# A second ordinary panel at the head of each feed-forward, splits of block sums in one piece, and weight sums held until the last square

## The chip, the cores and the metric

One core of a Trainium2 chip. The metric is the device time of one execution in microseconds. TensorE (PE) does matmuls, VectorE (DVE), ScalarE (ACT) and GpSimd (POOL) work on tiles of 128 partitions, and SP issues the loads. Each engine runs its own list of instructions in order; semaphores tie them together.

## What is computed

A block of two layers and a second block of one, in float32, over 512 tokens of width 1024: attention or a convolution or gated linear attention as the mixer of a layer, then a feed-forward. The change touches the three feed-forwards only, and what leads into them:

```python
def rmsnorm(x, g, eps=1e-6):
    xf = x.astype(jnp.float32)
    y = xf * lax.rsqrt(jnp.mean(xf * xf, axis=-1, keepdims=True) + eps)
    return (y * g.astype(jnp.float32)).astype(x.dtype)

def swiglu(h, w_gate, w_up, w_down):
    return (jax.nn.silu(h @ w_gate) * (h @ w_up)) @ w_down
...
        h = rmsnorm(x, ffn_norm[layer])
        x = x + swiglu(h, ffn_w_gate[layer], ffn_w_up[layer], ffn_w_down[layer])
```

The hidden width is 2816, which is 22 blocks of 128.

## The kernel before

Activations lie with their features on the partitions, 8 tiles of 128 x 512 (`x`). Every float32 product is made of three matmuls on halves of the mantissa: each operand is split into `hi` (a rounded copy, cast by ScalarE) and `lo` (the difference, by VectorE), and `hi·hi + lo·hi + hi·lo` is summed in PSUM. So each weight panel (128 x 2048, 1 MB) is loaded into one of two `raw` buffers, cast to `whi` by ScalarE and subtracted to `wlo` by VectorE. A load waits until the panel two before it is split. The mean square is not applied to the activations: `rstd` multiplies the results, so panels can start before it is known.

A feed-forward (`ffn`, f = 0, 1, 2) has 22 panels of gate and up weights, in two parts (12 and 10), each part followed by 8 down panels. Panel k holds the gate columns and the up columns of hidden block k. It is done in one of two ways:
- **ordinary** (panel 0): for each of the 8 feature tiles, gate and up, three matmuls of 512 columns: 48 in all, into two PSUM banks. Inside it stands the sum of squares (`sumsq`), from which ScalarE takes the root and VectorE the reciprocal (`inv`, `rstd`);
- **seven products** (panels 1 to 21): gate and up, and the first and second half of tokens, are treated as a 2 x 2 block product with seven products instead of eight, each of 4 x 3 matmuls of 256 columns: 84 in all, named B11, T1, B21, T2, B22, T3, T4 in the order of TensorE. They need sums of weights and sums of activations (**block sums**). GpSimd makes the weight sums of each panel with four additions (`weight_sums`; three can start once the panel has landed, the fourth after its `wlo`). ScalarE and VectorE split them (`hi_sum`, `lo_sum`, three of each a panel; `sw_hi`, `sw_lo`), ScalarE copies partial results between PSUM and SBUF (`take`), VectorE makes gate (`gate_first`, `gate_second`), up half (`up_second`, line 2050) and hidden (`hidden`), and T4 of a panel is issued after B11 of the next (`fourth`).

The block sums are made of x times its gain, once per feed-forward: `g12` and `n1` from tiles 0 to 3, `tt2`, `tt3`, `tt4` from tiles 4 to 7 (`summed`, line 1990, three sums a tile). They are split into `bt_hi` and `bt_lo` under the names T1, T2, T3; T4 goes into `act_hi` and `act_lo`.

The stage in front of a feed-forward (`late`) runs on VectorE and ScalarE while TensorE does the last matrix of the mixer: for each of 8 result tiles, x is updated (line 1998), squared and summed; the panel two ahead is split. Before the change `late` also does the block sums of tiles 4 and 5 and their splits T2 and T3 tile by tile (`part`), T1's split, then the first seven-product panel (`hi_panel`, `lo_panel`), the block sums of tiles 6 and 7 and their splits. `ffn` starts with panel 0 on TensorE; all that concerns it on VectorE (`whole_gate`, `whole_hidden`) is done inside step k = 1. The order on every engine is written out by hand, as these functions call one another. "Head" in what follows is the stretch from the first matmul of panel 0 to the start of steady work. "Panel 2" is the third one, and a panel's number is its k.

## Time and profile before

| | us |
|---|---|
| median of 3 runs | 1805.87 |
| lowest, highest | 1805.11, 1806.88 |
| profiled execution | 1802.89 |
| its span, first to last instruction | 1801.1 |
| TensorE busy | 1729.2 (96%) |
| VectorE busy | 1274.5 (71%) |
| ScalarE busy | 883.4 (49%) |
| GpSimd busy | 523.9 (29%) |
| three heads, first matmul of panel 0 | near 244, 785, 1374 |

The times come from executions of the whole program; the rows are of one profiled execution. Matmuls are pipelined: the durations shown overlap, and the distance of two starts is what one costs. TensorE's granted clock was 0.983 of full speed on average.

### The profile page before, as it was taken

What the parts mean: (1) busy time and instruction counts of PE and PEld (TensorE: products, weight loads), DVE (VectorE), ACT (ScalarE), POOL (GpSimd) and SP (SyncE); (2) the same over time, 40 slices, a digit from 0 to 9 for tenths busy, and PEclk for the clock granted to TensorE, in tenths of its full rate; (3) what the DMA queues carried; (4) which work ended last, traced back from release to release, by engine and by line L of the source; (5) the groups of instructions that cost most, each with busy time, mean ns of one, the idle gap of its engine ahead of it and who ended that gap; (6) DMA issues with size and microseconds to landing.
All of it is one profiled execution on the core that took longest, in us unless ns stands there. A gap on an engine that the chain in (4) does not pass through costs nothing. (4 is left out here: it accounts for less than half of the span.)

```text
span 1801.1 us, 27878 instructions
## 1 busy us (share of the span) xinstructions
PE 1729.2 (96%) x10773; PEld 1496.9 (83%) x10773; DVE 1274.5 (71%) x1792; ACT 883.4 (49%) x1355; POOL 523.9 (29%) x368
## 2 busy tenths in 40 slices
PE   7999989999999999989999999999998999999997
PEld 6776779988998865779988998788877998899876
DVE  8667688854875798688754776678758874477575
ACT  5338456732763312556732763433335673267342
POOL 1341125502540246225502540023301550255000
PEclk9899999999999999899999999999999999999998
...
DMA packets 284700, 169.01 MB, mean 94 GB/s; under 512 B 8288, under 2 KB 278528, under 8 KB 284576
## 3 DMA queue, kind: packets, MB, share of 16 engines
...
q8 instruction: 84, 1.38, 0.3%
...
## 5 line engine op out<-in xcount | busy, mean ns | idle before, releaser
L1036 PE MATMUL ps<-act_hi,whi 128*128 128x512 f32 x748 | 301.4, 403 | 22.3 <-DVE act_lo L1683 13.2
L1037 PE MATMUL ps<-act_lo,whi 128*128 128x512 f32 x748 | 294.3, 394 | 0.0
L1038 PE MATMUL ps<-act_hi,wlo 128*128 128x512 f32 x748 | 294.2, 393 | 0.0
L600 ACT ACTIVATE whi<-raw 128x2048 fp32r<-128x2048 f32 (+3 forms) x101 | 161.3, 1597 | 233.8 <-PE ps L1038 219.9
L1351 PE MATMUL ps<-act_hi,whi 128*128 128x256 f32 x756 | 215.4, 285 | 12.9 <-DVE t L2050 8.5
L1351 PE MATMUL ps<-act_lo,whi 128*128 128x256 f32 x756 | 213.6, 282 | 0.0
L1351 PE MATMUL ps<-act_hi,wlo 128*128 128x256 f32 x756 | 213.5, 282 | 0.0
L1651 DVE TENSOR_TENSOR wlo<-raw,whi 128x2048 fp32r<-128x2048 f32 (+3 forms) x93 | 183.1, 1969 | 38.0 <-ACT whi L600 37.7
L1036 PE MATMUL ps<-hid_hi,whi 128*128 128x512 f32 x528 | 209.8, 397 | 0.0
L1037 PE MATMUL ps<-hid_lo,whi 128*128 128x512 f32 x528 | 209.8, 397 | 0.0
L1038 PE MATMUL ps<-hid_hi,wlo 128*128 128x512 f32 x528 | 209.8, 397 | 0.0
L442 POOL TENSOR_TENSOR raw<-raw 128x512 f32<-128x512 f32 x63 | 82.7, 1313 | 402.3 <-DMA raw<-in_ffn_w_up_dram 240.6
L1036 PEld LDWEIGHTS ps<-act_hi,whi 128*128 128x128 f32 x748 | 142.4, 190 | 65.8 <-issue 27.6
L452 POOL TENSOR_TENSOR raw<-raw,ssum 128x512 f32<-128x512 f32 x63 | 102.2, 1623 | 228.0 <-DVE wlo L1964 228.0
L1038 PEld LDWEIGHTS ps<-act_hi,wlo 128*128 128x128 f32 x748 | 142.1, 190 | 30.6
L1037 PEld LDWEIGHTS ps<-act_lo,whi 128*128 128x128 f32 x748 | 142.7, 191 | 29.8 <-issue 1.2
L1964 DVE TENSOR_TENSOR wlo<-raw,whi 128x2048 fp32r<-128x2048 f32 x63 | 149.7, 2376 | 23.2 <-ACT whi L747 21.8
L1351 PEld LDWEIGHTS ps<-act_hi,whi 128*128 128x128 f32 x756 | 144.5, 191 | 15.9 <-issue 6.0
L1970 DVE TENSOR_TENSOR sw_lo<-ps,sw_hi 128x512 fp32r<-128x512 f32 x189 | 129.4, 684 | 28.7 <-ACT ps L761 28.4
L1351 PEld LDWEIGHTS ps<-act_lo,whi 128*128 128x128 f32 x756 | 144.1, 191 | 0.1
L1351 PEld LDWEIGHTS ps<-act_hi,wlo 128*128 128x128 f32 x756 | 144.1, 191 | 0.0
L1351 PE MATMUL ps<-bt_hi,sw_hi 128*128 128x256 f32 x504 | 143.1, 284 | 0.0
...
## 6 DMA issues: line engine op xcount, KB each, us to landing
...
```

What stands on the lines that cost most here:

```text
L442: pool.tensor_tensor(r[:, 2], r[:, 2], r[:, 3], ALU.add).then_inc(sem("w_sums"), 1)
L452: pool.tensor_tensor(r[:, 1], r[:, 1], ssum[:, 0], ALU.subtract).then_inc(sem("w_sums"), 1)
L600: act.activation(whi[:, n % 2, 0:cols], raw[:, n % 2, 0:cols], ACT.Copy).then_inc(hi_done, 1)
L1036: pe.matmul(out, lhs[0], rhs[0], start=start, stop=False)
L1037: pe.matmul(out, lhs[0], rhs[1], start=False, stop=False)
L1038: return pe.matmul(out, lhs[1], rhs[0], start=False, stop=stop)
L1351: ins = pe.matmul(out[:, 0:HALF], lhs, rhs[:, k], start=start and k == 0 and rhs is b_hi and lhs is w_hi, stop=k == Q4 - 1 and lhs is w_lo ...
L1651: ve.tensor_tensor(wlo[:, n % 2, a], raw[:, n % 2, a], whi[:, n % 2, a].bitcast(F32), ALU.subtract)\
L1964: ve.tensor_tensor(wlo[:, n % 2], raw[:, n % 2], whi[:, n % 2].bitcast(F32), ALU.subtract)\
L1970: ve.tensor_tensor(sw_lo[:, c], sum_bank(dn, c)[:, :], sw_hi[:, c].bitcast(F32), ALU.subtract)\
```

## The change

- Panel 1 of each feed-forward is done the ordinary way, like panel 0; seven products begin with panel 2. `seven(u)`, which counts seven-product panels, follows.
- Panel 1 is split by the plain `hi` and `lo` and has no weight sums. GpSimd starts the first weight sums of a feed-forward only when the last square before it has been added (`sq_added`).
- `late` no longer splits block sums, and makes only those of tiles 4 and 5. Those of tiles 6 and 7 come after `inv`, in step k = 0; T1, T2 and T3 are split in one piece each (128 x 1024), T1 after the root on ScalarE, T2 and T3 during panel 1; T4 in step k = 2.
- Gate and hidden of panel 0 are done in step k = 1, those of panel 1 in step k = 2, in other places of the queues.
- The single warm-up matmul ahead of B11 (line 1383) is gone.

The core of the diff:

```diff
@@ -235,7 +235,7 @@
         def seven(u):
-            return u - u // KF - 1
+            return u - 2 * (u // KF) - 2
         def sum_bank(dn, c):
@@ -434,8 +434,10 @@
                     for k in ks:
-                        if k == 0:
+                        if k < 2:
                             continue
+                        if k == 2:
+                            pool.wait_ge(sem("sq_added"), 8 * (FFN1, FFN2, FFN3)[f] + 8)
                         u, n = seven(KF * f + k), N0[up_ + part] + k - ks[0]
                         r = raw[:, n % 2].rearrange("p (c t) -> p c t", c=4)
@@ -791,15 +786,7 @@
-                    if Q4 <= k < KD - 2:
-                        part("T2", k - Q4)
-                        part("T3", k - Q4)
-                    if k == KD - 3:
-                        cast(flat2(combo("T1")[0]), flat2(n1[:, :, :]), "bt_hi", -1.0)
-                hi_panel(u0 + 1, n0 + 1)
-                for i in (2, 3):
-                    part("T2", i)
-                    part("T3", i)
+                hi(N0[up_ + "a"] + 1)
             late(0, FFN1, "mix", 0, "up1")
@@ -823,16 +810,25 @@
+                            act.wait_ge(sem("bt_sum"), 16 * f + 4)
+                            cast(flat2(combo("T1")[0]), flat2(n1[:, :, :]), "bt_hi", -1.0)
+                            continue
+                        if k == 1:
+                            hi_panel(u + 1, n + 1)
+                            silu(u - 1)
+                            act.wait_ge(sem("bt_sum"), 16 * f + 16)
+                            cast(flat2(combo("T2")[0]), flat2(tt2[:, :, :]), "bt_hi")
+                            cast(flat2(combo("T3")[0]), flat2(tt3[:, :, :]), "bt_hi")
+                            cast_hidden(u - 1)
                             hi_sum(u + 1, n + 1, dn, 0)
                             continue
-                        if k > ks[0] and k != 1:
+                        if k > ks[0]:
                             silu(u - 1)
                         if not first:
                             hi_sum(u, n, dn, 1)
                         take(u, dn, 0)
-                        if k == 1:
+                        if k == 2:
                             act.wait_ge(panel_done, n)
-                            act.wait_ge(sem("bt_sum"), 16 * f + 16)
                             cast(combo("T4")[0], tt4[:, :, :], "bt_hi")
                         if not first:
                             hi_sum(u, n, dn, 2)
@@ -1355,47 +1346,51 @@
-                        if u == KF * f + 1:
-                            pe.wait_ge(sem("bt_lo"), 10 * f + 10)
+                        if u == KF * f + 2:
+                            pe.wait_ge(sem("bt_lo"), 4 * f + 4)
                         pe.wait_ge(sem("c22_set"), seven(u) + 1)
                         product(up_banks(dn, u)[0], plain(n, 3), "T4", False, panel_done)
                     for k in ks:
                         u, n = KF * f + k, N0[up_] + k - ks[0]
                         a, b, c = up_banks(dn, u)
...
-                        if k == 0:
+                        if k < 2:
                             pe.wait_ge(split_done, n + 1)
+                            if k:
+                                pe.wait_ge(bank_free, T0[dn] + 4)
                             for kk in range(KD):
-                                if kk == 5:
+                                if k == 0 and kk == 5:
                                     sumsq(q)
-                                pe.wait_ge(*act_of(q)(kk))
+                                if k == 0:
+                                    pe.wait_ge(*act_of(q)(kk))
                                 for half, out in enumerate((a, b)):
                                     ins = mm3(out[:, :], slot(n, half * KD + kk, P), act_k(kk), kk == 0, kk == KD - 1)
                             ins.then_inc(panel_done, 1)
                             continue
                         w = seven(u)
                         pe.wait_ge(sem("up_split"), 3 * w + 1)
-                        if k == ks[0] + 1:
+                        if part == "b" and k == ks[0] + 1:
                             pe.wait_ge(bank_free, T0[dn] + 4)
-                        if u >= 2:
-                            pe.wait_ge(sem("up_summed"), 2 * (u - 1))
-                        if k == 1:
-                            pe.matmul(a[:, 0:HALF], plain(n, 0)(0)[0], combo("B11")[0][:, 0], start=True, stop=True)
+                        pe.wait_ge(sem("up_summed"), 2 * (u - 1))
                         product(c, plain(n, 0), "B11", True, sem("up_product"))
-                        if k > ks[0] and k != 1:
+                        if k > ks[0] and k != 2:
                             fourth(u - 1, n - 1)
-                        if k == 1:
-                            pe.wait_ge(sem("bt_lo"), 10 * f + 9)
+                        if k == 2:
+                            pe.wait_ge(sem("bt_lo"), 4 * f + 1)
                         product(b, plain(n, 2), "T1", True, sem("up_product"))
                         pe.wait_ge(sem("taken"), 3 * w + 1)
                         product(c, plain(n, 1), "B21", False, sem("up_product"))
                         pe.wait_ge(sem("up_split"), 3 * w + 2)
+                        if k == 2:
+                            pe.wait_ge(sem("bt_lo"), 4 * f + 2)
                         product(a, summed(0), "T2", False, sem("up_product"))
                         pe.wait_ge(split_done, n + 1)
                         pe.wait_ge(sem("taken"), 3 * w + 2)
                         product(b, summed(2), "B22", False, sem("up_product"))
                         pe.wait_ge(sem("up_split"), 3 * w + 3)
                         pe.wait_ge(sem("taken"), 3 * w + 3)
@@ -2006,25 +1993,15 @@
-                        summed(k - Q4)
-                        part("T2", k - Q4)
-                        part("T3", k - Q4)
+                        summed(f, q, k - Q4)
                     if k == KD - 1:
                         low_norm(q, k - 1)
                         low_norm(q, k)
                     add_square(q, k)
-                    if k == KD - 3:
-                        low(flat2(combo("T1")[1]), flat2(n1[:, :, :]), flat2(combo("T1")[0]), "bt_hi", 10 * f + 5,
-                            "bt_lo", -1.0)
                     if k == KD - 2:
                         for kk in range(KD - 2):
                             low_norm(q, kk)
-                lo_panel(u0 + 1, n0 + 1)
-                for i in (2, 3):
-                    summed(i)
-                for i in (2, 3):
-                    part("T2", i)
-                    part("T3", i)
+                lo(N0[up_ + "a"] + 1)
             late(0, FFN1, "mix", "up1")
@@ -2080,18 +2057,32 @@
                         if k == 0:
+                            inv(q)
+                            for i in (2, 3):
+                                summed(f, q, i)
                             continue
                         if k == 1:
-                            lo_sum(u, dn, 0)
-                            inv(q)
+                            whole_gate(u - 1, n - 1)
+                            lo_panel(u + 1, n + 1)
+                            whole_hidden(u - 1)
+                            low(flat2(combo("T1")[1]), flat2(n1[:, :, :]), flat2(combo("T1")[0]), "bt_hi", 4 * f + 1,
+                                "bt_lo", -1.0)
+                            low(flat2(combo("T2")[1]), flat2(tt2[:, :, :]), flat2(combo("T2")[0]), "bt_hi", 4 * f + 2,
+                                "bt_lo")
+                            low_hidden(u - 1)
+                            lo_sum(u + 1, dn, 0)
+                            low(flat2(combo("T3")[1]), flat2(tt3[:, :, :]), flat2(combo("T3")[0]), "bt_hi", 4 * f + 3,
+                                "bt_lo")
+                            continue
+                        if k == 2:
+                            whole_gate(u - 1, n - 1)
                             lo_sum(u, dn, 1)
-                            whole_gate(u - 1, n - 1)
                             lo_sum(u, dn, 2)
-                            low(combo("T4")[1], tt4[:, :, :], combo("T4")[0], "bt_hi", 10 * f + 10, "bt_lo")
+                            low(combo("T4")[1], tt4[:, :, :], combo("T4")[0], "bt_hi", 4 * f + 4, "bt_lo")
+                            whole_hidden(u - 1)
                             lo_panel(u + 1, n + 1)
+                            low_hidden(u - 1)
                             gate_first(u)
-                            whole_hidden(u - 1)
-                            low_hidden(u - 1)
```

What stands on VectorE between the x tiles 5 and 7 of the third `late` (`x<-x,ps` is the update of an x tile, `tt` a block sum, `bt_lo` a split of one, `act_lo` the split of x for panel 0), before:

```order
L1998 TENSOR_TENSOR x<-x,ps 128x512 [waits panel_done]
L1990 SCALAR_TENSOR_TENSOR tt<-x,par,n 128x256 [waits bt_sum,bank_free]
L1990 SCALAR_TENSOR_TENSOR tt<-x,par,g 128x256 [waits bt_sum]
L1990 SCALAR_TENSOR_TENSOR tt<-x,par,tt 128x256 [waits bt_sum]
L1681 TENSOR_TENSOR bt_lo<-tt,bt_hi 128x256 [waits bt_hi] x2
L1671 TENSOR_TENSOR sqacc<-sqacc,sq 128x512 [waits sq_added,sq_ready]
L1683 SCALAR_TENSOR_TENSOR bt_lo<-n,bt_hi 128x1024 [waits bt_hi]
L1651 TENSOR_TENSOR wlo<-raw,whi 128x2048 [waits hi_done]
L1998 TENSOR_TENSOR x<-x,ps 128x512 [waits tile_done]
L1671 TENSOR_TENSOR sqacc<-sqacc,sq 128x512 [waits sq_added,sq_ready,bank_free]
```

and now:

```order
L1985 TENSOR_TENSOR x<-x,ps 128x512 [waits panel_done]
L1975 SCALAR_TENSOR_TENSOR tt<-x,par,n 128x256 [waits bt_sum,bank_free]
L1975 SCALAR_TENSOR_TENSOR tt<-x,par,g 128x256 [waits bt_sum]
L1975 SCALAR_TENSOR_TENSOR tt<-x,par,tt 128x256 [waits bt_sum]
L1666 TENSOR_TENSOR sqacc<-sqacc,sq 128x512 [waits sq_added,sq_ready]
L1646 TENSOR_TENSOR wlo<-raw,whi 128x2048 [waits hi_done]
L1985 TENSOR_TENSOR x<-x,ps 128x512 [waits tile_done]
L1666 TENSOR_TENSOR sqacc<-sqacc,sq 128x512 [waits sq_added,sq_ready,bank_free]
L1678 SCALAR_TENSOR_TENSOR act_lo<-x,par,act_hi 128x512 [waits xhi] x6
L1985 TENSOR_TENSOR x<-x,ps 128x512 [waits panel_done]
```

Both rows of splits, three instructions, have gone from in front of `wlo` of panel 0.

VectorE in the third head, from the last block sum on (`sw_lo` is a split weight sum, `t<-ps,rstd` the gate of an ordinary panel, `t<-ps,t` its hidden), before:

```order
L1990 SCALAR_TENSOR_TENSOR tt<-x,par,tt 128x256 [waits bt_sum]
L1681 TENSOR_TENSOR bt_lo<-tt,bt_hi 128x256 [waits bt_hi] x4
L1970 TENSOR_TENSOR sw_lo<-ps,sw_hi 128x512 [waits sum_hi]
L1692 MEMSET sqacc 128x512 [waits std_ready]
L1693 RECIPROCAL rstd<-rstd 128x512
L1970 TENSOR_TENSOR sw_lo<-ps,sw_hi 128x512 [waits sum_hi,dve_seq]
L2064 TENSOR_TENSOR t<-ps,rstd 128x512 [waits panel_done]
L1970 TENSOR_TENSOR sw_lo<-ps,sw_hi 128x512 [waits sum_hi]
L1681 TENSOR_TENSOR act_lo<-tt,act_hi 128x4x256 [waits bt_hi]
L1964 TENSOR_TENSOR wlo<-raw,whi 128x2048 [waits hi_done]
```

and now:

```order
L1975 SCALAR_TENSOR_TENSOR tt<-x,par,tt 128x256 [waits bt_sum]
L2041 TENSOR_TENSOR t<-ps,rstd 128x512 [waits panel_done]
L1959 TENSOR_TENSOR wlo<-raw,whi 128x2048 [waits hi_done]
L2048 TENSOR_TENSOR t<-ps,t 128x256 [waits silu_ready]
L2048 TENSOR_TENSOR t<-ps,t 128x256
L1678 SCALAR_TENSOR_TENSOR bt_lo<-n,bt_hi 128x1024 [waits bt_hi]
L1676 TENSOR_TENSOR bt_lo<-tt,bt_hi 128x1024 [waits bt_hi]
L2054 TENSOR_TENSOR hid_lo<-t,hid_hi 128x512 [waits hidden_hi]
L1965 TENSOR_TENSOR sw_lo<-ps,sw_hi 128x512 [waits sum_hi]
L1676 TENSOR_TENSOR bt_lo<-tt,bt_hi 128x1024 [waits bt_hi]
L2041 TENSOR_TENSOR t<-ps,rstd 128x512 [waits panel_done]
L1965 TENSOR_TENSOR sw_lo<-ps,sw_hi 128x512 [waits sum_hi] x2
```

The reciprocal has moved ahead of the block sums, out of this piece; the splits of T1, T2 and T3 stand in one piece each between gate of panel 0 and gate of panel 1.

ScalarE in the third head, from the last square (`sq`) on, before:

```order
L606 ACTIVATE sq<-x 128x512 [waits sq_added]
L747 ACTIVATE whi<-raw 128x2048 [waits panel_done,w_sums]
L609 ACTIVATE bt_hi<-tt 128x256 [waits bt_sum] x4
L616 ACT_TABLE_LOAD
L616 ACTIVATE rstd<-ps,eps 128x512 [waits sumsq]
L756 ACTIVATE sw_hi<-ssum 128x512 [waits up_product,w_sums,std_ready]
L761 ACTIVATE ps<-ssum 128x512 [waits split_done]
L756 ACTIVATE sw_hi<-ssum 128x512 [waits up_product,w_sums]
L761 ACTIVATE ps<-ssum 128x512 [waits up_split]
L771 ACTIVATE ps<-ps 128x256 [waits up_product,hidden_lo,up_summed]
L609 ACTIVATE act_hi<-tt 128x4x256 [waits bt_sum,panel_done]
L756 ACTIVATE sw_hi<-raw 128x512 [waits up_product,w_sums]
```

and now:

```order
L608 ACTIVATE sq<-x 128x512 [waits sq_added]
L602 ACTIVATE whi<-raw 128x2048 [waits panel_done,raw_full1]
L618 ACT_TABLE_LOAD
L618 ACTIVATE rstd<-ps,eps 128x512 [waits sumsq]
L611 ACTIVATE bt_hi<-n 128x1024 [waits bt_sum,std_ready]
L749 ACTIVATE whi<-raw 128x2048 [waits panel_done,w_sums]
L799 ACT_TABLE_LOAD
L799 ACTIVATE t<-t 128x512 [waits up_summed]
L611 ACTIVATE bt_hi<-tt 128x1024 [waits bt_sum]
L611 ACTIVATE bt_hi<-tt 128x1024
L611 ACTIVATE hid_hi<-t 128x512 [waits hidden_set]
L758 ACTIVATE sw_hi<-ssum 128x512 [waits up_product,w_sums]
```

`whi` of the first panel of seven products stands behind the root; SiLU of panel 0 (`t<-t`) stands ahead of all casts of weight sums (`sw_hi`).

## Rows read from the trace of the kernel before

**Rows 1.** TensorE's waits, whole run: total us, times, longest us.

```profile
PE ps L1036 <- DVE act_lo L1683: 13.2, 4, 8.5
PE ps L1351 <- DVE t L2050: 8.5, 9, 2.0
PE ps L1351 <- DVE sw_lo L1970: 5.6, 3, 2.0
PE ps L1351 <- DVE bt_lo L1681: 5.4, 3, 1.9
...
PE ps L1351 <- ACT ps L771: 3.2, 3, 1.4
```

**Rows 2.** Timeline, TensorE: start us, us, line, tiles, [idle before <-releaser].

```profile
1373.87 0.47 PE L1036 MATMUL ps<-act_hi,whi 128*128 128x512 f32 x1 [1.54 <-DVE act_lo L1683]
...
1374.40 0.39 PE L1038 MATMUL ps<-act_hi,wlo 128*128 128x512 f32 x1
...
1380.53 0.39 PE L1038 MATMUL ps<-act_hi,wlo 128*128 128x512 f32 x1
1380.76 1.02 PE L1098 MATMUL ps<-sqacc,ones 128*128 128x512 f32 x2
...
1385.74 0.28 PE L1383 MATMUL ps<-act_hi,whi 128*128 128x256 f32 x1
...
1405.18 0.36 PE L1351 MATMUL ps<-act_hi,whi 128*128 128x256 f32 x1 [1.64 <-DVE t L2050]
...
1415.20 0.28 PE L1351 MATMUL ps<-act_hi,whi 128*128 128x256 f32 x1
```

**Rows 3.** Timeline, VectorE, third head.

```profile
1361.49 0.69 DVE L1998 TENSOR_TENSOR x<-x,ps 128x512 f32<-128x512 f32 x1 [1.92 <-PE ps L1038]
1362.21 1.32 DVE L1990 SCALAR_TENSOR_TENSOR tt<-x,par,n 128x256 f32<-128x256 f32 x1
...
1372.97 4.06 DVE L1683 SCALAR_TENSOR_TENSOR act_lo<-x,par,act_hi 128x512 fp32r<-128x512 f32 x6
...
1386.87 0.48 DVE L1990 SCALAR_TENSOR_TENSOR tt<-x,par,g 128x256 f32<-128x256 f32 x1
...
1391.74 0.48 DVE L1692 MEMSET sqacc<- 128x512 f32 x1
1392.14 3.29 DVE L1693 RECIPROCAL rstd<-rstd 128x512 f32<-128x512 f32 x1
...
1396.08 0.68 DVE L2064 TENSOR_TENSOR t<-ps,rstd 128x512 f32<-128x512 f32 x1
...
1397.27 1.38 DVE L1681 TENSOR_TENSOR act_lo<-tt,act_hi 128x1024 fp32r<-128x1024 f32 x1
1398.57 2.28 DVE L1964 TENSOR_TENSOR wlo<-raw,whi 128x2048 fp32r<-128x2048 f32 x1
...
1404.63 0.41 DVE L2050 TENSOR_TENSOR t<-t,ps 128x256 f32<-128x256 f32 x1
```

**Rows 4.** Timeline, ScalarE, third head.

```profile
1366.27 1.91 ACT L600 ACTIVATE whi<-raw 128x2048 fp32r<-128x2048 f32 x1
...
1389.11 0.69 ACT L616 ACTIVATE rstd<-ps,eps 128x512 f32<-128x512 f32 x1
1389.84 0.63 ACT L756 ACTIVATE sw_hi<-ssum 128x512 fp32r<-128x512 f32 x1
...
1390.89 0.61 ACT L756 ACTIVATE sw_hi<-ssum 128x512 fp32r<-128x512 f32 x1
...
1391.93 0.34 ACT L771 ACTIVATE ps<-ps 128x256 f32<-128x256 f32 x1
```

**Rows 5.** Timeline, GpSimd, third head.

```profile
1363.32 1.36 POOL L446 TENSOR_TENSOR ssum<-raw 128x512 f32<-128x512 f32 x1
```

**Rows 6.** Stretch: us, busy PE, PEld, DVE, ACT, POOL, PEclk, DMA, GB/s.

```profile
1398.00:1400.00 2.00, 2.00 (x15) 2.00 (x14) 2.00 (x2) 0.57 (x2) 0.00 (x0) 0.68 0.61 178
1400.00:1402.00 2.00, 2.00 (x10) 1.88 (x10) 1.85 (x4) 0.12 (x1) 1.07 (x1) 0.50 1.17 312
```

36 lines of the change are left out of this document (12 added, 24 removed).

## The prediction, made before the changed kernel had run

> **What bounds the kernel now.** I read the waits of TensorE first, then the heads of the three feed-forwards in the timelines. TensorE is busy nearly all of the span, so only its idle time and the kind of its matmuls count. Of that idle time a good part stands at three places that look alike. [rows 1]: three of the four waits for `act_lo` (4.7 us without the one of 8.5), three for `sw_lo` (5.6), three for `bt_lo` (5.4), three for the copy by ScalarE of line 771 (3.2), and of the nine waits for the sum of line 2050 the three longest (some 5.4 of 8.5) lie at the heads. Together 24 us, 8 a head. I work on the third head; the others stand in the same order at nearly the same pace.
>
> The reader should see a row of dependences, not a busy engine. TensorE waits 1.54 us for `act_lo` and starts the ordinary panel at 1373.87; at 1385.74 it starts the first panel of seven products and waits in it; at 1405.18, after 1.64 more, comes the fourth-block product of that panel, and from there on 84 matmuls of 256 columns take 1415.20 − 1405.18 = 10.0 us, which is 0.119 each, without a wait [rows 2]. VectorE is what it waits for. It is late before the head because its sums for `tt` took 1.32 us instead of 0.48 [rows 3] while GpSimd ran sums of 1.36 us [rows 5]: two engines on SBUF operands take turns. It is late again in the head, where the reciprocal (3.29 us) stands in front of all that needs `rstd`, and the splits of block sums and weights are queued round it.
>
> **Part 1, the wait before the head.** New: GpSimd's three sums start only after the last square, and six pieces of splits leave VectorE's queue ahead of the first panel. VectorE takes x tile 5 at 1361.5, as before. Then: x 0.7, three sums at a pitch of 0.52 (1363.8), the square 0.7 (1364.4). ScalarE's `whi` (1.9 us [rows 4]) starts after its square at 1362.9 and ends at 1364.8, `wlo` takes 2.3: 1367.1. The next x tile was ready on TensorE at 1366.8 (24 matmuls of 0.227 before the end of the panel at 1372.3), so x, square and first cast put the first `act_lo` at 1369.8, ahead of the 1372.3 at which TensorE comes free. The panel starts at 1372.3 instead of 1373.9: **1.6 us** gained. Six `act_lo` (4.06) end at 1373.2, the last two at 1375.4, the last square at 1376.1. The added wait holds nothing but GpSimd's own sums: 1.36, one behind VectorE's `wlo` and a third, done by 1382.5; who waits for them is ScalarE's `whi` of panel 2, which can't start before panel 0 ends (1384.2). That cover is 1.7 us thick. On the queue of the loads nothing waits longer: the load of panel 3 now follows `wlo` of panel 1, 15 us earlier than it did.
>
> **Part 2, matmuls.** The second panel becomes 48 matmuls of 512 columns. From 1374.40 to 1380.53 there are 27, 0.227 each [rows 2], so 10.9 us, against 84 × 0.119 = 10.0 and one warm-up matmul of 0.1 before: **0.8 us a head more**. The Trainium skill, "TensorE: Matmul & The Clock Gate", section "Wait — 56ns, not 53.3ns?", gives N ÷ 2.4 GHz plus 2.5 ns: by it this term would be 10.36 − 9.17 = 1.2 us; both widths run some 10 ns slower in this trace, and the rows decide.
>
> **Part 3, what the second ordinary panel hides.** Panel 0 takes 11.9 us with the sum of squares inside it (1373.87 to 1385.74), so it ends at 1384.2, and panel 1 at 1395.1. The sum of squares starts 6.9 us into panel 0 (1380.76 before), at 1379.2, and takes 1.0; the root 0.7 more: 1380.9. VectorE is ready for it: `wlo` of panel 1 waits until 1377.5 for GpSimd and ends at 1379.7. From 1380.9 VectorE does, in its new order and with the durations of [rows 3]:
> - zeroing and reciprocal, 3.7: 1384.6. Six sums at 0.52: 1387.7 (GpSimd's three sums are over). Gate of panel 0, 0.6: 1388.3. `wlo` of panel 2, 2.2: 1390.5. Hidden of panel 0, 0.7: 1391.2.
> - split of T1. GpSimd started its fourth sum at 1390.5 and holds until 1391.9; the split, some 1.2 (one of the same size was 1.38, partly in GpSimd's way), ends at 1393.1. GpSimd's next sum goes first, to 1394.4; split of T2 1395.7; `hid_lo` and the split of weight sum 0, 0.6 each: 1396.9; split of T3 1398.1; gate of panel 1, 0.6: 1398.7.
>
> All but the last 3.6 us lie under panel 1. TensorE then does B11 and T1 of panel 2 (2.8 us, to 1397.9) and must wait for ScalarE's copy, which is queued behind SiLU of panel 1: 0.6 after the gate, then the pair of casts (1389.84 to 1390.89, so 1.05), then the copy 0.35: 1400.8. **Wait 1: 2.9 us.** It stands where `take` stood before (1.4). B21 and T2 run to 1403.7. ScalarE meanwhile has the cast of T4 (some 1.0), a pair (1.05), `whi` (1.8) and a copy (0.35): 1405.0. **Wait 2: 1.3 us.** B22, T3 and the next panel's B11 run to 1409.3. VectorE: T4's split to 1404.8, hidden 1405.5, `wlo` of panel 3 1407.7, then `hid_lo`, three gate steps (0.35, 0.4, 0.45, or 1.1 if GpSimd is in the way) and the sum of line 2050, 0.4: 1410.3. **Wait 3: 1.1 us**, the fourth-block product starts at 1410.4.
>
> The same product stood at 1415.2 [rows 2]; what follows is the same steady stretch. Gain 4.8 us a head by these steps. I take 0.3 off for the clock (below): **4.5 us, three heads 13.5 us**. In the two other heads the steps are the same; nothing else in the program changes.
>
> **The clock.** Behind three waits the granted clock was 0.68 in 1398 to 1400 and 0.50 in 1400 to 1402, that is 1.2 of 2.4 GHz [rows 6]; it cost 2 × 0.32 + 2 × 0.50 = 1.6 us. After the change wait 1 is longer than any now, so I count on one such fall in each head. It would lie over B21 to T3, where waits 2 and 3 take up most of it; hence only 0.3. The same page of the Trainium skill, section "The HAM clock gate", says idleness throttles the clock and activity releases it; by it the fall would stay, too.
>
> **Unknown costs.** The turns with GpSimd: none of them met (splits at 1.2, no waits) gives 1408.6, or 6.6 a head; two more sums of 1.36 met, each moving the whole chain, and the clock's 1.6 paid in full, gives 0.5 to 2 a head. I take the middle way, since the sums of [rows 3] are hit one for one. Range of the forecast 3 × 2 to 3 × 6.6: 6 to 20 us.
>
> **Rivals.**
> - Less is gained (VectorE's chain behind the root is the bound, and every split meets GpSimd): 1.2 to 3.3 a head, 4 to 10 us, around 1799. For it: the chain from 1380.9 to 1398.7 is full, nothing in it can slip. Against: GpSimd has only five sums in these 20 us.
> - More is gained: 5.6 a head and over, 17 us or more, around 1786. For it: T1 and T2 may slip in between GpSimd's sums.
> - Nothing is gained: the hold keeps GpSimd's sums so late that they fall in the six sums of VectorE (0.9 each, 5.4 us), which eats the 4.8. Time 1804 to 1808. Against: they should be over at 1383, VectorE starts at 1384.6.
> - Slower: the gate of panel 1 comes after 1403.5 instead of 1398.7. Then copy, casts and `whi` shift with it and the fourth-block product is behind 1415.2. It needs the six sums and three of the splits to meet GpSimd (5.4 + 4.1); with the clock's 1.6 that is 6 us a head too many, so (9.5 + 1.6 − 4.8) × 3 = 19 us slower at worst, 1825; at half of it around 1812.
>
> **Numbers.** Profiled execution: 1802.89 us with a span of 1801.1; the runs' median, 1805.87, is 3.0 above. The gain is a difference of spans, so 1805.87 − 13.5 = **1792.4** (span near 1787.6). Chances: forecast (10 to 17 us gained) 0.50, less 0.20, more 0.18, nothing 0.05, slower 0.07. About 0.2%, 3.6 us, is what a measurement can tell from no change: faster 0.88, same 0.05, slower 0.07. The range leaves out nothing-and-slower and the tail of "more": 1786 to 1800.
>
> **What would show it.** Right: no wait for `act_lo` at the three heads; none between the two ordinary panels; the first wait at a copy of ScalarE in the third panel; waits at the heads down from 24 to some 16 us; the three x-tile sums at 0.48; 256-column matmuls fewer by 3 × 85. Wrong: a wait in front of the third panel (then `wlo` or the gate is late), sums of 1.4 us behind the reciprocal (then the hold has only moved the turns), or waits of over 0.5 us further on in each feed-forward, which would mean that the head's lag is carried along.

## The result and the profile after

The changed kernel takes **1783.16 us** (median, 1782.07 to 1790.93) against 1805.49 for the one before (four executions of each; 1805.87 was the median of the first three of the one before): ratio 0.9886, 95% interval 0.9856 to 0.9916. In a second comparison, with more executions, it was 1784.17 against 1806.05 (0.9880, 0.9861 to 0.9900). That is 22 us gained (21.9 in the second comparison, interval 18 to 25), where I had forecast 13.5 and had let the range end at 1786. The sign was right; the forecast gain was some 40% too small, and the time fell below the range.

TensorE's waits over the whole run of the kernel after (total us, times, longest us), which answer to [rows 1]:

```profile
PE ps L1027 <- DVE act_lo L1678: 8.8, 1, 8.8
PE ps L1342 <- ACT ps L773: 6.9, 3, 2.3
PE ps L1342 <- DVE t L2027: 4.4, 9, 0.6
...
PE ps L1342 <- ACT t L773: 1.1, 1, 1.1
```

Of the first row of [rows 1] only the wait at the start of the run is left; `sw_lo` and `bt_lo` are gone from the list, `ps` by ScalarE has grown from 3.2 to 6.9, and the sum for the fourth block has halved (line 2027, before 2050; six of its nine waits, 0.5 each, lie behind the heads in both kernels). Three more waits for another `act_lo` (4.2 us, 5.0 before) lie outside the heads. At the three heads together 24 us of waits have become 9.2: a copy 2.3 in each, the sum 0.35 to 0.6, and 1.1 once. I had forecast 16.

The third head of the kernel after on TensorE: the last matmul of the second ordinary panel, the first of the first panel of seven products (now panel 2), its two waits, and the first matmul of the down projection (start us, us, line, tiles, [idle before <-releaser]). It answers to [rows 2]:

```profile
1387.53 0.39 PE L1029 MATMUL ps<-act_hi,wlo 128*128 128x512 f32 x1
1387.76 0.28 PE L1342 MATMUL ps<-act_hi,whi 128*128 128x256 f32 x1
...
1393.07 0.38 PE L1342 MATMUL ps<-act_hi,whi 128*128 128x256 f32 x1 [2.30 <-ACT ps L773]
...
1402.25 0.35 PE L1342 MATMUL ps<-act_hi,whi 128*128 128x256 f32 x1 [0.35 <-DVE t L2027]
...
1492.63 0.40 PE L1027 MATMUL ps<-hid_hi,whi 128*128 128x512 f32 x1
```

VectorE at the same head, which answers to [rows 3]:

```profile
1354.41 0.69 DVE L1985 TENSOR_TENSOR x<-x,ps 128x512 f32<-128x512 f32 x1 [2.59 <-PE ps L1029]
1355.14 0.48 DVE L1975 SCALAR_TENSOR_TENSOR tt<-x,par,n 128x256 f32<-128x256 f32 x1
...
1359.85 0.69 DVE L1985 TENSOR_TENSOR x<-x,ps 128x512 f32<-128x512 f32 x1
...
1377.55 0.48 DVE L1975 SCALAR_TENSOR_TENSOR tt<-x,par,n 128x256 f32<-128x256 f32 x1
...
1384.02 1.89 DVE L1678 SCALAR_TENSOR_TENSOR bt_lo<-n,bt_hi 128x1024 fp32r<-128x1024 f32 x1
1385.83 2.31 DVE L1676 TENSOR_TENSOR bt_lo<-tt,bt_hi 128x1024 fp32r<-128x1024 f32 x1
...
1389.26 1.21 DVE L1676 TENSOR_TENSOR bt_lo<-tt,bt_hi 128x1024 fp32r<-128x1024 f32 x1
1390.39 0.68 DVE L2041 TENSOR_TENSOR t<-ps,rstd 128x512 f32<-128x512 f32 x1
...
1401.70 0.41 DVE L2027 TENSOR_TENSOR t<-t,ps 128x256 f32<-128x256 f32 x1
```

x tile 5 stands at 1354.41 here and at 1361.49 before, so 7.08 added to a time of this head gives the scale of the prediction. The fourth-block product of the first panel of seven products starts at 1409.33 on that scale: forecast 1410.4, before 1415.20. The block sum of tile 5 takes 0.48 instead of 1.32, and x tile 6 follows x tile 5 after 5.44 us instead of 9.45.

ScalarE between the gate of panel 1 and the two copies that TensorE waited for or could have waited for, and GpSimd's sums of which two lie in the way of the splits (they answer to [rows 4] and [rows 5]):

```profile
1391.11 0.63 ACT L799 ACTIVATE t<-t 128x512 f32<-128x512 f32 x1 [5.33 <-DVE t L2041]
1391.64 0.61 ACT L758 ACTIVATE sw_hi<-ssum 128x512 fp32r<-128x512 f32 x1
1392.16 0.58 ACT L763 ACTIVATE ps<-ssum 128x512 f32<-128x512 f32 x1
1392.68 0.33 ACT L773 ACTIVATE ps<-ps 128x256 f32<-128x256 f32 x1
...
1396.73 0.36 ACT L773 ACTIVATE t<-ps 128x256 f32<-128x256 f32 x1
```

```profile
1368.84 1.29 POOL L444 TENSOR_TENSOR raw<-raw 128x512 f32<-128x512 f32 x1 [85.66 <-DVE sqacc L1666]
1370.21 3.20 POOL L448 TENSOR_TENSOR ssum<-raw 128x512 f32<-128x512 f32 x1
...
1383.51 1.31 POOL L454 TENSOR_TENSOR raw<-raw,ssum 128x512 f32<-128x512 f32 x1 [8.72 <-DVE wlo L1959]
1384.90 2.15 POOL L444 TENSOR_TENSOR raw<-raw 128x512 f32<-128x512 f32 x1
```

The granted clock behind the wait of 2.3 us (stretch: us, busy PE, PEld, DVE, ACT, POOL, PEclk, DMA, GB/s), which answers to [rows 6]:

```profile
1392.00:1394.00 2.00, 0.93 (x7) 0.94 (x8) 0.69 (x1) 2.00 (x5) 0.39 (x1) 0.96 0.00 0
1394.00:1396.00 2.00, 2.00 (x11) 2.00 (x11) 0.97 (x2) 2.00 (x3) 0.90 (x1) 0.50 0.00 0
1396.00:1398.00 2.00, 2.00 (x15) 2.00 (x14) 2.00 (x4) 1.54 (x3) 0.00 (x0) 0.68 0.42 117
```

It falls to 0.50, that is 1.2 of 2.4 GHz, as before, right behind the wait.

**A yardstick.** Whole times spread by 10 us from one execution to the next, so I measured each head by itself: from the start of x tile 5 on VectorE to the first matmul of the down projection on TensorE. In the kernel after that is 1492.63 − 1354.41 = 138.22. The profiles of all kernels that follow, in the order of their experiments; the last column says where inside heads 1, 2 and 3 the granted clock fell to 0.50 ("none": it did not):

| kernel | head 1 | head 2 | head 3 | clock falls, us behind x tile 5 |
| --- | --- | --- | --- | --- |
| before, first trace | 144.34 | 144.06 | 144.02 | 37, 28, 37 |
| after, first trace | 138.20 | 138.22 | 138.22 | none, 39, 39 |
| again (after, second trace) | 138.17 | 138.18 | 138.19 | none, 39, 40 |
| base_repeat (before, second trace) | 145.70 | 145.99 | 143.55 | 45, 45, 37 |
| no_hold | 138.20 | 138.20 | 138.18 | none, 40, none |
| hold_only | 144.87 | 144.91 | 144.11 | 27, 29, 27 |
| copy_first | 136.89 | 137.61 | 137.68 | none, 41, 43 |
| t3_late | 137.05 | 137.05 | 137.05 | none |
| both_moves | 136.59 | 136.60 | 137.34 | none, none, 42 |
| splits_ahead | 136.39 | 136.54 | 136.40 | none |
| ahead_no_hold | 137.46 | 137.60 | 137.43 | none |
| ahead_take1 | 136.42 | 136.55 | 136.41 | none |
| ahead_takes | 136.59 | 136.58 | 136.58 | none |
| ahead_best | 136.00 | 136.14 | 135.99 | none |

### The profile page after: what moved, and what is told of

It reads as the page before. It is cut to its first block, busy times and chain, and to the rows that moved or that the text cites. A ratio compares the mean times of both kernels' runs of the same rounds, so it can differ in the third digit from the quotient of the medians.

```text
span 1789.1 us, 27531 instructions
## 1 busy us (share of the span) xinstructions
PE 1734.1 (97%) x10662; PEld 1498.1 (84%) x10662; DVE 1251.9 (70%) x1756; ACT 867.4 (48%) x1310; POOL 516.9 (29%) x356
## 4 chain that ended last, share of the span: by engine, by line
PE 47%; DVE 6%; issue 1%; ACT 1%; POOL 0%; DVEq 0%; POOLq 0%; ACTq 0%
PE ps L1342 21%; PE ps L1027 8%; PE ps L1028 8%; PE ps L1029 8%; DVE wlo L1646 1%; DVE rstd L1688 1%; PE ps L1535 0%; ACT whi L602 0%; DVE act_lo L1678 0%; DVE act_lo L1676 0%; DVE wlo L1959 0%; DVE tt L1975 0%; DVE x L2439 0%; DVE bt_lo L1676 0%; DVE at L2305 0%
## 5 line engine op out<-in xcount | busy, mean ns | idle before, releaser
L1027 PE MATMUL ps<-act_hi,whi 128*128 128x512 f32 x796 | 320.0, 402 | 16.9 <-DVE act_lo L1678 8.8
L1028 PE MATMUL ps<-act_lo,whi 128*128 128x512 f32 x796 | 313.8, 394 | 0.0
L1029 PE MATMUL ps<-act_hi,wlo 128*128 128x512 f32 x796 | 313.0, 393 | 0.0
L1646 DVE TENSOR_TENSOR wlo<-raw,whi 128x2048 fp32r<-128x2048 f32 (+3 forms) x96 | 191.3, 1993 | 42.7 <-ACT whi L602 42.5
L1342 PE MATMUL ps<-act_hi,whi 128*128 128x256 f32 x720 | 205.5, 285 | 11.2 <-ACT ps L773 6.9
L1342 PE MATMUL ps<-act_hi,wlo 128*128 128x256 f32 x720 | 204.1, 283 | 0.0
L1342 PE MATMUL ps<-act_lo,whi 128*128 128x256 f32 x720 | 204.0, 283 | 0.0
L1959 DVE TENSOR_TENSOR wlo<-raw,whi 128x2048 fp32r<-128x2048 f32 x60 | 141.4, 2356 | 20.0 <-ACT whi L749 19.1
L1965 DVE TENSOR_TENSOR sw_lo<-ps,sw_hi 128x512 fp32r<-128x512 f32 x180 | 123.2, 684 | 31.5 <-ACT ps L763 31.3
L1342 PE MATMUL ps<-bt_hi,sw_hi 128*128 128x256 f32 x480 | 135.8, 283 | 0.0
```

Source lines behind the costliest of these rows:

```text
L1027: pe.matmul(out, lhs[0], rhs[0], start=start, stop=False)
L1028: pe.matmul(out, lhs[0], rhs[1], start=False, stop=False)
L1029: return pe.matmul(out, lhs[1], rhs[0], start=False, stop=stop)
L1342: ins = pe.matmul(out[:, 0:HALF], lhs, rhs[:, k], start=start and k == 0 and rhs is b_hi and lhs is w_hi, stop=k == Q4 - 1 and lhs is w_lo ...
L1646: ve.tensor_tensor(wlo[:, n % 2, a], raw[:, n % 2, a], whi[:, n % 2, a].bitcast(F32), ALU.subtract)\
L1959: ve.tensor_tensor(wlo[:, n % 2], raw[:, n % 2], whi[:, n % 2].bitcast(F32), ALU.subtract)\
```

## Experiments

### Where 22 us come from: both kernels once more

> The changed kernel once more, for its median, its spread and a second trace. From x tile 5 to the fourth-block product of the second panel of seven products a head took 54.0, 53.8 and 53.7 us before and 47.8 in each after: 6.2 + 5.9 + 5.9 = 18.0 us. Theory A: that is all the change gives; the 22.3 us of the medians hold some 4 us of low clock outside the heads, which differs from run to run, and with more rounds the gain comes to 17 to 20 us. Theory B: the change also gives 4 us between the heads; then the gain stays at 21 to 23 us, and in two traces of like clock the stretches from a head's end to the next head's x tile 5 are shorter after than before by more than 1 us each.

> The kernel before, run as it is, for a second trace of it and for what two builds of one kernel differ by. Expected: ratio 1.000 within 0.002, heads of 53.7 to 54.0 us as in the first trace, and the low clock of the attention stage (85 to 150 us) not the same as in the first trace. If its heads differ by more than 0.5 us from the first trace, the 18.0 us read from one pair of traces is not sure.

Measured: again 1784.17 (ratio 0.9880, 0.9861 to 0.9900), base_repeat 1806.32 (0.9998, 0.9984 to 1.0012). Neither theory holds as I wrote it. The gain stayed at 21.9, which speaks against A. But the stretches between the heads have not become shorter, which speaks against B: from the first down matmul of a feed-forward to the next x tile 5, or to the end, they are 396.84, 444.31 and 295.59 us before and 396.87, 444.60 and 296.47 after.

What I had not thought of is in base_repeat: heads 1 and 2 of the kernel before take 1.4 and 1.9 us longer than in its first trace, while the kernel after takes the same in all six of its heads, to 0.05 us. TensorE's waits in head 1 of base_repeat, x tile 5 at 236.39:

```profile
276.73 0.36 PE L1351 MATMUL ps<-act_hi,whi 128*128 128x256 f32 x1 [1.19 <-DVE t L2071]
280.27 0.36 PE L1351 MATMUL ps<-act_hi,whi 128*128 128x256 f32 x1 [1.88 <-DVE t L2050]
```

And the granted clock, first behind these, then in head 3 (x tile 5 at 1370.79):

```profile
280.00:282.00 2.00, 1.73 (x11) 1.76 (x12) 1.22 (x3) 2.00 (x5) 1.13 (x1) 0.76 0.03 8
282.00:284.00 2.00, 2.00 (x11) 2.00 (x11) 1.61 (x4) 2.00 (x3) 1.44 (x2) 0.50 0.00 0
1406.00:1408.00 2.00, 1.09 (x7) 1.09 (x8) 2.00 (x3) 1.99 (x3) 1.07 (x1) 0.86 0.04 8
1408.00:1410.00 2.00, 2.00 (x11) 2.00 (x11) 2.00 (x2) 0.07 (x1) 0.00 (x0) 0.50 0.78 222
```

In head 3, and in the three heads of the first trace, the clock falls 28 to 37 us behind x tile 5, ahead of the last wait, and the waits that follow absorb it. In head 3 here the wait of 1.19 is gone and the last one is 1.03 (most of the 0.85 by which that is shorter than 1.88 has another reason, below):

```profile
1414.01 0.36 PE L1351 MATMUL ps<-act_hi,whi 128*128 128x256 f32 x1 [1.03 <-DVE t L2050]
```

In heads 1 and 2 it falls 45 us behind x tile 5, behind the last wait, and is paid in full: from the end of that wait to the first down matmul these two heads take 101.8 us, the other four of the kernel before 100.3. So a fall there costs 1.5 us. The rest of the differences is the time of the fourth-block product itself, 43.2 to 44.2 us behind x tile 5. It follows VectorE's step of line 2044 just ahead of the sum, which took 1.33, 1.09 and 1.10 us in the first trace and 1.13, 1.27 and 0.42 in this one: in all but the last a sum of GpSimd had begun before it. The kernel after has heads without any fall (its head 1) and heads with one (2 and 3, 39 us behind x tile 5), and both take 138.2: at that place the waits that follow cover the fall.

So the gain of a head depends on where the clock falls in the kernel *before*, and two traces of it don't say how often it falls at the dear place. Paired by how the attention stage ran (in some executions the clock is lower at 130 to 150 us, 0.66 instead of 0.96 and 0.87 in its two halves, and the first head starts 4 us later), the two kernels differ by 1810.0 − 1789.1 = 20.9 us (base_repeat, after), of which the heads are 20.6, and by 1801.1 − 1782.6 = 18.5 us (before, no_hold below), of which the heads are 17.8. The mean of the two traces is 6.4 a head, 19.2 in all. That lies inside the interval of the medians, 18 to 25, and what is left of the 21.9, 2.7 us, I can't place.

### The wait of GpSimd

```
 for k in ks:
     if k < 2:
         continue
-    if k == 2:
-        pool.wait_ge(sem("sq_added"), 8 * (FFN1, FFN2, FFN3)[f] + 8)
```

> The changed kernel without the wait of GpSimd for the last square: its first three weight sums run as soon as the weights are there, as before. Theory A (the hold keeps GpSimd out of VectorE's way): the block sums of the last tiles take 1.3 us instead of 0.48 again, TensorE waits 1 to 1.5 us for act_lo at each head, and the kernel is 3 to 5 us slower than the changed one. Rival (the hold only moves the turns; the second ordinary panel alone leaves slack at the head, since six splits have left VectorE's queue): the wait for act_lo stays away or under 0.3 us, and the time is within 1 us of the changed kernel.

The other way round, the kernel before with this wait ahead of its first sum (at `k == 1`):

> The kernel before with one line added: GpSimd's first sum of each feed-forward waits for the last square. Everything else as before. Theory A: the sums of VectorE ahead of the head fall to 0.48 us, the panel starts up to 1.6 us earlier at each head, up to 4.8 us in all. Rival: the first panel of seven products, which needs these sums early (its whi stands ahead of the root), waits longer for sw_lo and bt_lo by as much, since GpSimd's sums now meet VectorE's splits inside the head: 0 to 1.5 us gained, or some lost.

Measured: no_hold 1784.50 (0.9880, 0.9862 to 0.9898), heads 138.2 as with the wait. hold_only 1804.88 (1.0006, 0.9995 to 1.0016), heads 144.1 to 144.9. The rival holds both times: **the hold gives nothing** in either kernel. But the rival's reason is not the right one either, as GpSimd's rows in no_hold show, with x tile 5 and the first block sum of it on VectorE ahead:

```profile
1348.71 0.69 DVE L1983 TENSOR_TENSOR x<-x,ps 128x512 f32<-128x512 f32 x1 [2.59 <-PE ps L1027]
1349.43 0.48 DVE L1973 SCALAR_TENSOR_TENSOR tt<-x,par,n 128x256 f32<-128x256 f32 x1
...
1360.89 3.01 DVE L1676 SCALAR_TENSOR_TENSOR act_lo<-x,par,act_hi 128x512 fp32r<-128x512 f32 x2
1363.83 1.77 DVE L1664 TENSOR_TENSOR sqacc<-sqacc,sq 128x512 f32<-128x512 f32 x1
```

```profile
1360.35 1.29 POOL L442 TENSOR_TENSOR raw<-raw 128x512 f32<-128x512 f32 x1 [82.59 <-DMA raw<-in_w_gate_upffn_dram]
1361.72 1.63 POOL L446 TENSOR_TENSOR ssum<-raw 128x512 f32<-128x512 f32 x1
```

GpSimd starts 11.6 us behind x tile 5, released by the load and by nothing else. In the kernel before, the sum of [rows 5], the second of its three, stood 1.8 us behind x tile 5. The reason is the second ordinary panel: GpSimd's first sums now belong to panel 2, whose weights land later, so they miss the block sums of tile 5 by themselves. They meet the last `act_lo` and the last square instead (3.01 for two instead of 1.51, 1.77 instead of 0.68), and nobody waits for those.

In hold_only the block sums of tile 5 are at 0.48 too and the panel starts on time. What was gained there was lost behind it, as the rival said: the first panel of seven products is already panel 1, and its `whi` needs the first of the held sums. It starts 17.5 us behind x tile 5, no earlier than before (17.3), and its `wlo` takes 2.91 us beside the second and third sum instead of 2.29. The panel in front of it now ends 1.8 us earlier, so `bt_lo` is waited for 4.3 us instead of 1.8:

```profile
1379.41 1.91 ACT L749 ACTIVATE whi<-raw 128x2048 fp32r<-128x2048 f32 x1 [2.32 <-POOL raw L444]
```

```profile
1390.48 0.58 PE L1353 MATMUL ps<-bt_hi,whi 128*128 128x256 f32 x1 [4.34 <-DVE bt_lo L1683]
...
1405.71 0.36 PE L1353 MATMUL ps<-act_hi,whi 128*128 128x256 f32 x1 [1.17 <-DVE t L2052]
```

### What makes the wait of 2.3 us

ScalarE's order in the first panel of seven products:

```
-if k > ks[0]:
-    silu(u - 1)
-if not first:
-    hi_sum(u, n, dn, 1)
-take(u, dn, 0)
+if k == 2:
+    take(u, dn, 0)
+    hi_sum(u, n, dn, 1)
+    silu(u - 1)
+else:
+    if k > ks[0]:
+        silu(u - 1)
+    if not first:
+        hi_sum(u, n, dn, 1)
+    take(u, dn, 0)
```

> The changed kernel, with ScalarE's copy for the first panel of seven products and the cast of its second weight sum moved ahead of the SiLU of panel 1. TensorE's first wait of a head (2.3 us, ended by that copy) then no longer hangs on VectorE's chain and the gate of panel 1. Theory A (the queue order on ScalarE makes the wait, and it is on the path): that wait falls from 2.3 to under 0.3 us; VectorE's next splits then set the second wait, which grows to 0.5 to 1.5 us; 1 to 2 us gained a head, 3 to 6 us in all: 1778 to 1781. Rival (VectorE's chain sets the fourth-block product whatever the copy does, because hidden, wlo and the gate steps of VectorE come at the same times): the wait only moves to the sum behind it and the time stays within 1 us of the changed kernel.

VectorE's order instead:

```
 if k == 1:
     ...
     lo_sum(u + 1, dn, 0)
-    low(flat2(combo("T3")[1]), flat2(tt3[:, :, :]), flat2(combo("T3")[0]), "bt_hi", 4 * f + 3,
-        "bt_lo")
     continue
 if k == 2:
     whole_gate(u - 1, n - 1)
+    low(flat2(combo("T3")[1]), flat2(tt3[:, :, :]), flat2(combo("T3")[0]), "bt_hi", 4 * f + 3,
+        "bt_lo")
     lo_sum(u, dn, 1)
```

> The changed kernel, with the split of T3 on VectorE moved behind the gate of panel 1 (ScalarE's order as in the changed kernel). The gate comes 1.2 us earlier, so the copy too. Theory A (VectorE's chain behind the reciprocal sets the first wait): the wait of 2.3 us falls to 1.0 to 1.2 and nothing later grows, since T3 is needed some 8 us later: 1.1 us a head, 3 us in all. Rival: the sums of VectorE are late anyway further on, so that the waits for them (0.5 us a head now) grow by what the first loses: 0 to 1 us gained.

> The changed kernel with both moves: copy and second weight cast ahead of SiLU on ScalarE, T3's split behind the gate on VectorE. If the copy's place alone removes the first wait, T3's place adds at most 0.5 us a head to that: time within 1.5 us of the kernel with the copy first. If the two add up (VectorE's chain is the bound even then), it is 1 us a head or more faster than either.

Measured: copy_first 1782.55 (0.9862, 0.9848 to 0.9877), t3_late 1783.74 (0.9876, 0.9861 to 0.9892), both_moves 1782.35 (0.9867, 0.9851 to 0.9884). By the heads the gains against 138.2 are 2.4, 3.5 and 4.1 us in all; by the medians they are 1.6, 0.4 and 1.8 against 1784.17, each uncertain by some 3 us. The runs can't rank the three, and the heads only where the clock ran alike.

TensorE's only wait between panel 1 and the fourth block in the third head of copy_first, and the granted clock behind it:

```profile
1390.27 0.35 PE L1347 MATMUL ps<-act_hi,sw_hi 128*128 128x256 f32 x1 [2.29 <-ACT t L773]
```

```profile
1392.00:1394.00 2.00, 2.00 (x12) 2.00 (x11) 2.00 (x4) 0.49 (x1) 1.18 (x1) 0.50 0.98 269
```

and TensorE's waits in that head of t3_late, where the clock doesn't fall:

```profile
1384.49 0.39 PE L1342 MATMUL ps<-act_hi,whi 128*128 128x256 f32 x1 [1.15 <-ACT ps L773]
1388.67 0.36 PE L1342 MATMUL ps<-act_hi,sw_hi 128*128 128x256 f32 x1 [1.06 <-ACT t L773]
1393.66 0.36 PE L1342 MATMUL ps<-act_hi,whi 128*128 128x256 f32 x1 [0.49 <-DVE t L2027]
```

In copy_first the wait is gone at its place and back at full length two products on: the second copy still stands behind SiLU, the cast of T4 and `whi`. Its theory expected 0.5 to 1.5 us there. In t3_late the wait halves and 1.15 us a head is gained, as theory A said.

Which of the two moves gives more is not to be read from the sums of three heads, since t3_late had no fall of the clock in any head and copy_first had one in two, 41 and 43 us behind x tile 5, near the end of its one long wait or behind it. Those two heads take 0.7 and 0.8 us more than its head 1. Among heads without a fall copy_first takes 136.89, which is 1.3 us gained, inside the 1 to 2 of its theory A; t3_late takes 137.05 (1.15 gained) and both_moves 136.59 and 136.60 (1.6). With the copy first, T3's place gives 0.3 a head more, in head 1 without a fall and in head 3 with one in both kernels; the expectation allowed at most 0.5. **The two moves take away mostly the same wait**: the copy stands behind VectorE's gate of panel 1 by way of SiLU, and either a shorter chain to the gate or a copy that doesn't wait for it makes it come earlier.

### One half of the change without the other

`splits_ahead` keeps the two ordinary panels and the hold, and puts the splits of the block sums back where they were:

```
 elif k < KD - 2:
     summed(f, q, k - Q4)
+    piece(f, "T2", k - Q4)
+    piece(f, "T3", k - Q4)
 ...
+if k == KD - 3:
+    low(flat2(combo("T1")[1]), flat2(n1[:, :, :]), flat2(combo("T1")[0]), "bt_hi", 10 * f + 5,
+        "bt_lo", -1.0)
 ...
 if k == 1:
     whole_gate(u - 1, n - 1)
     lo_panel(u + 1, n + 1)
     whole_hidden(u - 1)
-    low(flat2(combo("T1")[1]), flat2(n1[:, :, :]), flat2(combo("T1")[0]), "bt_hi", 4 * f + 1,
-        "bt_lo", -1.0)
-    low(flat2(combo("T2")[1]), flat2(tt2[:, :, :]), flat2(combo("T2")[0]), "bt_hi", 4 * f + 2,
-        "bt_lo")
+    for i in (2, 3):
+        piece(f, "T2", i)
+        piece(f, "T3", i)
     low_hidden(u - 1)
     lo_sum(u + 1, dn, 0)
-    low(flat2(combo("T3")[1]), flat2(tt3[:, :, :]), flat2(combo("T3")[0]), "bt_hi", 4 * f + 3,
-        "bt_lo")
```

with the same on ScalarE (`piece` is the `part` of the kernel before), and one wait of TensorE for the hidden of panel 0 that the split of T1 had stood for.

> The changed kernel's two ordinary panels, but with the splits of T1 and of the first half of T2 and T3 where they stood in the kernel before, in pieces ahead of the first panel; only the last two pieces of T2 and T3 are made during panel 1. This divides the change in two. Theory A (the six pieces taken from VectorE's queue, not the hold on GpSimd, removed the wait for act_lo): that wait is back with some 1.5 us a head, +4.5 us in all, while VectorE's chain behind the reciprocal is 2 to 4 us shorter, so that the first wait of 2.3 us shrinks to under 0.5, -5.5 us in all: within 2 us of the changed kernel, with the waits in other places. Rival (the act_lo wait came from the turns with GpSimd, which the hold keeps away here too): act_lo stays under 0.3 us and the kernel is 4 to 6 us faster than the changed one.

Measured: **1779.01** (0.9849, 0.9836 to 0.9861), heads 136.4 to 136.5. This is 5 us faster than the changed kernel: by the heads 1.75 each, 5.3 in all. The rival holds, in the time and in the place: `act_lo` isn't waited for. All of TensorE's waits from 1320 to 1430 us:

```profile
PE ps L1350 <- ACT t L773: 1.1, 1, 1.1
PE ps L1350 <- DVE t L2047: 0.5, 1, 0.5
PE ps L1350 <- ACT ps L773: 0.5, 1, 0.5
```

x tile 6 comes 7.19 us behind x tile 5 here, 1.75 later than in the changed kernel and 2.26 earlier than before, and there is room for it ahead of the panel. So the early splits (five instructions on VectorE, not six: two pieces each of T2 and T3, and T1) cost nothing where they stood. Moved into VectorE's chain behind the reciprocal they cost 1.75 us a head: there T1, T2 and T3 take 5.4 us, two of them beside a sum of GpSimd, where the four late pieces of splits_ahead take 3.2. With the hold, everything in the change but the move of the splits gives 144.6 − 136.4 = 8.2 us a head, and that move takes a fifth of it back.

Was it the hold that kept `act_lo` quiet here?

> The kernel with two ordinary panels and the early pieces ahead of the head (splits_ahead), without the wait of GpSimd for the last square. The wait for act_lo before a head (1.5 us before) is gone in every kernel where either GpSimd held its sums or the pieces had left VectorE's queue. Theory A (it takes both: the three block sums at 1.3 to 1.4 us instead of 0.48, 2.7 us, and the pieces, 1.8 us, on top of the same queue): act_lo is waited for again, 1.0 to 1.6 us at each head, and the kernel is 3 to 5 us slower than splits_ahead. Rival (the earlier load of the next panel or the order of the wlo splits removed it): no wait for act_lo, and the time of splits_ahead within 1 us.

Measured: 1783.83 (0.9873, 0.9853 to 0.9893), heads 137.4 to 137.6. The time is what theory A said (by the heads 1.05 each, 3.1 in all), the place is not: the block sums of tile 5 are at 0.48 as in no_hold, x tile 6 again comes 7.18 us behind, no `act_lo` is waited for at a head. GpSimd's sums meet the last `act_lo` and the last square, and now the sum of squares waits for those:

```profile
1366.23 2.82 DVE L1685 SCALAR_TENSOR_TENSOR act_lo<-x,par,act_hi 128x512 fp32r<-128x512 f32 x2
1368.98 1.78 DVE L1673 TENSOR_TENSOR sqacc<-sqacc,sq 128x512 f32<-128x512 f32 x1
```

```profile
1370.81 1.13 PE L1095 MATMUL ps<-sqacc,ones 128*128 128x512 f32 x2 [0.84 <-DVE sqacc L1673]
```

The hold is worth 1.1 us a head where the pieces stand ahead of the panel, and nothing in the kernel as changed.

### Getting past both kernels

Three more on top of splits_ahead, all of them in the first panel of seven products. In ahead_take1 the second copy comes ahead of `whi`; ahead_takes adds to it the order of copy_first:

```
+if k == 2:
+    take(u, dn, 1)
 if k < ks[-1]:
     hi_panel(u + 1, n + 1)
```

> splits_ahead with ScalarE's second copy of the first panel of seven products moved ahead of the whi cast of the next panel (1.9 us), in that panel only. Theory (TensorE's second wait, 1.1 us, is ScalarE's queue and lies on the path): it falls to 0 to 0.3, what follows comes up by 0.8 us or less, since VectorE's sum for the fourth block is then the last to be ready: 1.5 to 3 us faster than splits_ahead in all. Rival (the third wait, for VectorE's sum, takes all of it, from 0.5 to 1.5 us): within 0.5 us.

> As the kernel with the second copy moved, and also the first copy and the cast of the second weight sum ahead of the SiLU of panel 1. Theory: the first wait (0.5 us a head) goes as well; VectorE's chain of gate, hidden, wlo and gate steps is the bound: another 0 to 0.5 us a head, 0 to 1.5 us in all. Rival: SiLU and with it hidden and the casts behind it come later, the wait for VectorE's sum grows, and it is no faster or 1 us slower.

Measured: ahead_take1 1780.29 (0.9857, 0.9839 to 0.9875), ahead_takes 1779.72 (0.9849, 0.9832 to 0.9866); heads 136.4 and 136.6. Both rivals hold: nothing is gained. The wait of 1.1 us stood one product later, presumably for the third copy ("issue" is the profile's word where it names no releaser), and the sum came no earlier:

```profile
1386.63 0.36 PE L1353 MATMUL ps<-bt_hi,sw_hi 128*128 128x256 f32 x1 [0.98 <-issue]
1390.33 0.36 PE L1353 MATMUL ps<-act_hi,whi 128*128 128x256 f32 x1 [0.62 <-DVE t L2050]
```

The last one puts the third copy ahead of the cast of hidden as well, and on VectorE:

```
 if k == 2:
     ...
     lo_panel(u + 1, n + 1)
-    low_hidden(u - 1)
     gate_first(u)
     gate_second(u)
     continue
 if k > ks[0]:
     up_second(u - 1)
+    if k == 3:
+        low_hidden(u - 2)
```

> As ahead_take1, with the third copy of that panel also ahead of the cast of hidden, and VectorE's split of hidden of panel 1 moved behind the fourth-block sum. From x tile 5 to the first down matmul a head takes 136.4 to 136.5 us in splits_ahead and in ahead_take1: moving the second copy only moved the 1.1 us wait one product on. Theory (VectorE's unbroken chain from the third weight sum to the fourth-block sum is the bound, so only the split of hidden, 0.6 us, counts; the copy alone would give nothing): 135.8 to 136.0 a head, 1.5 to 2 us faster in all, 1777 to 1779. Rival (the third copy's place was the bound): 135.4 or less a head, 3 us or more in all.

Measured: **1778.21** (0.9836, 0.9823 to 0.9850), heads 136.0 to 136.1: 0.4 a head by taking 0.6 out of VectorE's chain, near the low end of the theory and far from the rival. The third copy's place has no visible part in it: `wlo` of panel 3 starts 41.2 us behind x tile 5 in this kernel and in ahead_take1, and VectorE goes on from there without a pause in both. The missing 0.2 is in one of the gate steps, 0.96 instead of 0.76:

```profile
1388.44 0.96 DVE L2047 TENSOR_TENSOR t<-t,rstd 128x256 f32<-128x256 f32 x1
```

It is the fastest kernel of this study, 30 us under the one before in the same comparison. Under the changed one it is 5 to 6 us by the medians of different comparisons and 6.5 by the heads.

## Why the prediction was too small

The mechanism behind the root was right. What failed is the size, 4.5 us a head where the heads show 6.4: it was read from a single head, its waits 1 to 3 were put too long and a fall of the clock was charged that cost nothing. In part 1 the size was right and the cause wrong.

- **The sum was made on one head of one trace.** It took head 3 of the first trace as the size of all heads ("In the two other heads the steps are the same"). For the waits that was right. For the clock it wasn't: heads 1 and 2 of base_repeat are 1.4 and 1.9 us longer, since the fall came behind the last wait, where it costs 1.5. Mean of its two traces: 144.6, against 144.0 for the head I used. That is 1.8 us of the missing gain.
- **Part 1, the wait before the head.** The 1.6 us are there and the panel starts where forecast, but by luck, since the step named the wrong causes: the hold, and the pieces (it counted six, there are five). no_hold and splits_ahead each take one away and no wait for `act_lo` comes back; ahead_no_hold takes both away and still none does. What removed it is that GpSimd's sums now belong to a panel whose weights land 11 us later. (In the kernel before, the hold would have removed it too, as hold_only shows.) I had written that the load of panel 3 follows earlier and stopped there; the load of panel 2, which releases the sums, I never timed.
- **Part 2, matmuls.** Right: panel 1 is 48 matmuls at 0.227 between its start and 1387.76, which is 1394.84 on the forecast's scale (forecast 1395.1). By the rule of the Trainium skill, "TensorE: Matmul & The Clock Gate", section "Wait — 56ns, not 53.3ns?", the two panels would have differed by 1.2 us (an estimate from its 2.5 ns) instead of 0.8. The trace keeps its own pitches, 0.227 and 0.119, and doesn't agree with it.
- **Part 3, the schedule behind the root.** Right in its order and nearly so in its times. On the forecast's scale the six sums ended at 1387.6 (forecast 1387.7), the split of T1 at 1393.0 (1393.1), T2 at 1395.2 (1395.7), the gate of panel 1 at 1398.15 (1398.7). GpSimd's turns did cost what was put in: T1 1.89 and T2 2.31, against 1.21 for T3.
- **Waits 1 to 3, the term that was mis-sized.** Put at 2.9, 1.3 and 1.1 us, 5.3 together, they were too long by 1.1 a head, 3.2 in all. The fourth-block product waits for VectorE's sum, and VectorE reached that sum at 1408.8 instead of 1409.9: 0.55 of it stands at the gate of panel 1, 0.4 more between that gate and the end of T4's split (1403.9, forecast 1404.8), and the rest of the chain ran nearly as forecast. Head 1 has no fall of the clock and waits of 2.3, 1.05 and 0.56; heads 2 and 3 have a fall, which stretches the products where the second wait stood, and waits of 2.3 and 0.35 to 0.38. Both come to the product 47.8 us behind x tile 5.
- **The clock, 0.3 a head.** It was 0, for the same reason: a head with a fall and one without take 138.2 alike. 0.9 in all.
- **Added up:** 1.8 + 3.2 + 0.9 = 5.9, which leads from 13.5 to the 19.2 of the heads (19.4 by this rounding). The remaining 2.7 of the medians stays open, inside their uncertainty.
- **The rivals.** "More is gained", 0.18 at 17 us and over, is what happened, but not because T1 and T2 slipped between GpSimd's sums: they were hit both. Less, nothing and slower did not occur. The six sums behind the reciprocal took 0.48 each, so the mechanism of "nothing is gained" wasn't at work either; hold_only shows another way in which the hold eats its own gain, with `whi` behind the held sums.
- **The range.** The steps' own upper end was 20 us, time 1786, with a trace 3 us under the median as its base. It held no room for heads of the kernel before that differ from one execution to the next. The 19.2 us of the heads would still lie in it, just under its end; the 22 of the medians do not, and the part that carries them over it is the part that stays open.
